# The inverse of the chunk matrices as pairs of 64x64 tiles: one step of a hybrid diffusion backbone

## The reference, cut to what matters

```
low = jnp.where(strict, jnp.einsum('bhncd,bhnsd->bhncs', kb, k) * decay, 0.0)
tmat = lax.linalg.triangular_solve(eye + low, jnp.broadcast_to(eye, low.shape), left_side=True, lower=True)
u = tmat @ vb
w = tmat @ (kb * jnp.exp(g)[..., None])
def step(s, inp):                      # over the chunks
    v_new = u_i - w_i @ s
    o_i = q_i @ s + qk_i @ v_new
    s = s * gl_i[..., None, None] + jnp.einsum('bhcd,bhce->bhde', k_i, v_new)
```

## Time and profile before

| | us |
|---|---|
| median of 3 runs | 8628.4 |
| lowest, highest | 8619.2, 8630.4 |
| span of the profiled execution | 8614.4 |
| PE busy with matmuls | 6895.8 (80%) |
| PE busy with weight loads | 5819.8 (68%) |
| DVE busy | 4241.4 (49%) |
| ACT busy | 1628.0 (19%) |
| POOL busy | 290.5 (3%) |

### The profile page before, as it was taken

The page is one execution under the profiler, slowest core; times in us unless marked ns, Lnnn a source line. Parts: engine busy times, 40 slices in busy tenths (PEclk is TensorE's granted clock), DMA queues, the critical chain, the costliest instruction groups (busy, mean ns, idle before and its releaser), DMA issues. The chain is left out here.

```text
span 8614.4 us, 112116 instructions
## 1 busy us (share of the span) xinstructions
PE 6895.8 (80%) x44860; PEld 5819.8 (68%) x44860; DVE 4241.4 (49%) x7492; ACT 1628.0 (19%) x2928; POOL 290.5 (3%) x260
## 2 busy tenths in 40 slices
PE   7788888888798677798945676699678887888698
PEld 1666666666698555697944565599566666666698
DVE  0446666666434422434156666433546666666433
ACT  0211111111222122323221111222211111111322
POOL 0000000000000000000000000000000000000000
PEclk9899999999899777899977787799888888888899
DMA  6221111110221200221311000121110000000121
GB/s 244 78 76 38 38 38 39 38 38 32 73 73 47 77 16 16 74 78 49 113 51 37 25 19 20 64 70 60 65 50 9 9 9 9 9 9 3 68 78 56
DMA packets 96935, 429.11 MB, mean 50 GB/s; under 512 B 16041, under 2 KB 26537, under 8 KB 64873
## 3 DMA queue, kind: packets, MB, share of 16 engines
q1 hardware_dynamic: 83248, 392.92, 12.9%
q10 hardware_dynamic: 13248, 30.15, 0.9%
HBM read 374.03 MB, written 49.26 MB: 49 GB/s over the span
## 5 line engine op out<-in xcount | busy, mean ns | idle before, releaser
L343 PE MATMUL bank<-src_hi,ring_hi 128*128 128x320 f32 x4032 | 936.6, 314 | 358.9 <-DVE ring_lo L335 354.9
L343 PE MATMUL bank<-src_lo,ring_hi 128*128 128x320 f32 x4032 | 933.3, 313 | 7.4 <-issue 7.4
L343 PEld LDWEIGHTS bank<-src_hi,ring_hi 128*128 128x128 f32 x4032 | 688.4, 192 | 362.8 <-issue 358.2
L343 PE MATMUL bank<-src_hi,ring_lo 128*128 128x320 f32 x4032 | 932.5, 313 | 0.0
L343 PEld LDWEIGHTS bank<-src_lo,ring_hi 128*128 128x128 f32 x4032 | 688.6, 192 | 7.8 <-issue 7.8
L343 PEld LDWEIGHTS bank<-src_hi,ring_lo 128*128 128x128 f32 x4032 | 687.6, 191 | 0.0
L335 DVE TENSOR_TENSOR ring_lo<-ring,ring_hi 128x2048 fp32r<-128x2048 f32 x190 | 434.9, 2289 | 508.6 <-ACT ring_hi L331 507.7
L735 PE MATMUL bank<-xx,y 128*128 128x128 f32 x3200 | 522.6, 286 | 75.5 <-DVE y L768 56.3
L779 DVE TENSOR_TENSOR xx<-bank,xx 128x512 f32<-128x512 f32 x600 | 414.7, 691 | 289.0 <-PE bank L739 289.0
L768 DVE TENSOR_TENSOR y<-bank,const 128x256 f32<-128x256 f32 x1000 | 416.1, 421 | 283.3 <-PE bank L727 277.4
L727 PE MATMUL bank<-xx,lt 128*128 128x128 f32 x3200 | 501.5, 288 | 26.1 <-DVE xx L779 26.1
(11 more groups left out here) (354 smaller groups left out, 11469.4 us busy)
## 6 DMA issues: line engine op xcount, KB each, us to landing
ring<-w_mlp SPq DMA_DIRECT2D x128, 1024.0 KB, 4.8
mod_ring<-w_mod SPq DMA_DIRECT2D x24, 2048.0 KB, 7.7
mod_slab<-w_mod SPq DMA_DIRECT2D x24, 2048.0 KB, 7.6
ring<-rw_wrkv SPq DMA_DIRECT2D x24, 1024.0 KB, 4.7
ring<-dn_win SPq DMA_DIRECT2D x16, 1024.0 KB, 5.2
rkv<-stage ACTq DMA_DIRECT2D x48, 320.0 KB, 2.2
rkv<-rkv SPq DMA_DIRECT2D x48, 320.0 KB
rows<-dn_rows SPq DMA_DIRECT2D x8, 1920.0 KB, 6.8
```

Of the source, the lines that this page charges most:

```text
L343: last = self.nc.tensor.matmul(acc[h][:, 0:HALF], wt[:, n % 2, k, m * P:(m + 1) * P], x[:, k, h * HALF:(h + 1) * HALF], start=first and q ...
```

## The change

The zeros beside the diagonal blocks are no longer kept. `lt`, `xx`, `y`, `x0` and `tt` have 128 rows of 64 columns: rows 0 to 63 are the block of one direction, rows 64 to 127 that of the other. Each product of two 128x128 matrices becomes two products of 64x64 (SIDES), one on rows 0 to 63 into partitions 0 to 63, one on rows 64 to 127 into partitions 64 to 127 of the same PSUM bank. The DVE instructions of the inverse have half as many columns; their masks are tables of 64 columns. The start's transposes are products with the identity, thus two records each. The product from which `lt` comes is formed in 64 columns too: in time mixing by 64x64 tiles on the rows of one head, in the delta heads by 128x64 tiles over all rows, and its mask there runs by sides (64 partitions of 256 columns) where it ran by heads (128 partitions of 256 columns). The product with `tt` in the chains runs as pairs of tiles of 64x64 with all its 128 columns moving. All waits of PE ahead of such tiles become `wait_alone`.

```diff
-    t[:, K_L0:K_L0 + P] = (row // 2 == col // 2) & (col > row)
+    row, col = r[:, None] % C, r[None, :C]
+    t[:, K_SPC:K_SPC + C] = col > row
+    t[:, K_L0:K_L0 + C] = (row // 2 == col // 2) & (col > row)
+    t[:, K_IDC:K_IDC + C] = row == col
...
+SIDES = (slice(0, C), slice(C, P))
...
 def invert_first_pe(pe, nc, g, s, w, i, j, h):
-    pe.wait_ge(s["first_t"], group_at(i, j, "first_t", h + 1))
+    wait_alone(pe, s["first_t"], group_at(i, j, "first_t", h + 1), s["passed"])
     for n in range(2):
-        last = nc.tensor.transpose(w.y_bank[h][:, (2 + n) * P:(3 + n) * P], w.x0[h][:, 1, n, :], g.ident)
+        for er in SIDES:
+            last = nc.tensor.matmul(w.y_bank[h][er, (2 + n) * C:(3 + n) * C], w.x0[h][er, 1, n, :], g.ident[er, er],
+                                    start=True, stop=True)
...
-            pe.wait_ge(s["xx_ready"], group_at(i, j, "xx_ready", 2 * lv + h + 1))
+            wait_alone(pe, s["xx_ready"], group_at(i, j, "xx_ready", 2 * lv + h + 1), s["passed"])
...
             for n in range(2):
-                last = nc.tensor.matmul(w.y_bank[h][:, n * P:(n + 1) * P], w.lt[:, j % 2, 2 * h + n, :], xx[h][:, 0, n, :],
-                                        start=True, stop=True)
+                for er in SIDES:
+                    last = nc.tensor.matmul(w.y_bank[h][er, n * C:(n + 1) * C], w.lt[er, j % 2, 2 * h + n, :],
+                                            xx[h][er, 0, n, :], start=True, stop=True)
...
-            pe.wait_ge(s["ly_ready"], group_at(i, j, "ly_ready", 2 * lv + h + 1))
             if lv == 0 and j:
-                pe.wait_ge(s["inv_ready"], group_at(i, j - 1, "inv_ready", h + 1))
+                wait_alone(pe, s["inv_ready"], group_at(i, j - 1, "inv_ready", h + 1), s["passed"])
+            wait_alone(pe, s["ly_ready"], group_at(i, j, "ly_ready", 2 * lv + h + 1), s["passed"])
             for n in range(2):
-                last = nc.tensor.matmul(w.x_bank[h][:, (2 + n) * P:(3 + n) * P], w.y[:, h, n, :], xx[h][:, 1, n, :],
-                                        start=True, stop=True)
+                for er in SIDES:
+                    last = nc.tensor.matmul(w.x_bank[h][er, (2 + n) * C:(3 + n) * C], w.y[er, h, n, :], xx[h][er, 1, n, :],
+                                            start=True, stop=True)
...
-                nc.vector.tensor_tensor(both, w.x_bank[h][:, :], before, ALU.add).then_inc(s["xx_ready"], 1)
+                nc.vector.tensor_tensor(both, w.x_bank[h][:, 0:4 * C], before, ALU.add).then_inc(s["xx_ready"], 1)
...
-        w.lt, w.xx, w.y = sb("lt", 2, GROUP, P), sb("xx", 2, 2, 2, P), sb("y", 2, 2, P)
+        w.lt, w.xx, w.y = sb("lt", 2, GROUP, C), sb("xx", 2, 2, 2, C), sb("y", 2, 2, C)
...
                         hr = slice(C * hh, C * (hh + 1))
-                        for q, (left, right) in enumerate(((bt, at_), (kt, at_), (kt, rt), (bt, rt))):
+                        for n in range(2):
+                            u = 2 * jg + n
+                            for e, er in enumerate(SIDES):
+                                nc.tensor.matmul(bank[4 + 2 * hh][er, n * C:(n + 1) * C], bt[hr, u, e, :], at_[hr, u, e, :],
+                                                 start=True, stop=True)
+                        for q, (left, right) in enumerate(((kt, at_), (kt, rt), (bt, rt)), 1):
...
-                        pe.wait_ge(s["x_out"], at(i, 2 * STEPS, 2 * n + 2))
+                        wait_alone(pe, s["x_out"], at(i, 2 * STEPS, 2 * n + 2), s["passed"])
                         for hh, uk in enumerate(uks):
-                            last = nc.tensor.matmul(bank[1][:, hh * P:(hh + 1) * P], w.tt[:, uk, :],
-                                                    xs[:, hh, :].unsqueeze(1).to_broadcast([P, 2, C]), start=True, stop=True)
+                            for er in SIDES:
+                                last = nc.tensor.matmul(bank[1][er, hh * P:(hh + 1) * P], w.tt[er, uk, :],
+                                                        xs[er, hh, :].unsqueeze(1).to_broadcast([C, 2, C]),
+                                                        start=True, stop=True)
...
+                            if b == 0:
+                                for er in SIDES:
+                                    last = nc.tensor.matmul(bank[0][er, n * C:(n + 1) * C], k2[:, hh, u, er], k2[:, hh, u, er],
+                                                            start=True, stop=True)
...
-                        pe.wait_ge(s["tmp_out"], at(i, STEPS, n + 1))
+                        wait_alone(pe, s["tmp_out"], at(i, STEPS, n + 1), s["passed"])
```

84 lines of the change are left out of this document (49 added, 35 removed).

## The result

The changed kernel takes 8176.4 us (median of 3 runs, 8171.3 to 8185.3) against 8628.4: ratio 0.948, 95% interval 0.9464 to 0.9498. The forecast was 8050: of 582 us less, span to span, 445 came. The result lies in the stated range (7940 to 8450), but 16 us above the range that the forecast's own bounds gave (7940 to 8160). The page of the changed kernel first: span, busy time, the queue that fetches instructions, and the two lines of y and x products.

A forecast was written before the change was run, and what follows sets the result against it. It took TensorE's instruction stream to bound the inverse's levels. The inverses save 601 us and the chains add 19, so the span falls from 8614.4 to 8032; with 14 around it 8046, stated as 8050. Range 7940 to 8450.

The forecast's parts named there:

- Price of a pair, 0.12: In the inverse, a pair of 64x64 products takes 0.12 us where one 128x128 product took 0.22; bounds 0.11 and 0.22.
- Rival (b): The two tiles of a pair don't overlap: 8560 us, or 8700 with dearer waits and pairs; chance 0.12.
- DVE, 415 and 283 ns: In the inverse, VectorE's sum falls from 691 to 415 ns and the mask from 421 to about 283.
- the ring: Half 0's loop in a quiet level: x products, sum, wait, y products, mask, wait; 2.20 us against 3.28 before.
- The wait, 0.135: In the inverse, PE's separate wait makes loads start 0.135 us behind DVE's end; bounds 0.05 and 0.22.
- The levels, 3.73, 3.74, 2.20, 4.34, 1.64: Time-mixing heads, us for each level of a group after the change; before, modelled 5.15, 5.07, 3.15, 6.35, 2.33.
- the walk: Following all 25 levels of a block by dependence: 105.5 us before, 74.6 after; delta heads 94.2 and 67.5.
- rival (c): Instruction supply to TensorE doesn't hold 46 per us in the inverse; at 30 the kernel takes 8730 us; chance 0.05.
- rival (a): TensorE's clock in the inverse is no longer granted in full; near 8400 us; chance 0.12.
- A: Theory from the experiments, not the prediction: the clock falls because the narrow tiles leave PE too thinly used.
- The chain, +19: The tt product's change of form and wait add 16 us (0 to 32) in 160 chain steps, 3 in 40 delta steps.
- Around the span, 14 us: Before the change, the runs' median 8628.4 us stood 14 above the profiled span; added to 8032 to give 8046.

The follow-up runs named there:

- e4: Changed kernel with each of the 800 VectorE sums writing its 256 columns twice, so 512 as before; 8279 us, ratio 0.9607 to the kernel before.
- e3: Kernel before with only the waits of the inverse changed, each made an instruction of its own; 8653 us, ratio 1.0036 to the kernel before.
- e8: Changed kernel with 8 more TensorE instructions per level that only count up a semaphore; 8176 us, ratio 0.9480 to the kernel before.
- e9: Changed kernel with 64 semaphore-counting TensorE instructions ahead of the loop of each time-mixing phase, shifting the code; 8121 us, ratio 0.9416 to the kernel before.
- e1: Changed kernel with unread 128x128 products over 96 columns put into TensorE's idle spots of the inverse; 8346 us, ratio 0.9686 to the kernel before.
- e6: Changed kernel with unread pairs of 64x64 bf16 tiles of 256 columns as fills in TensorE's idle spots of the inverse; 8156 us, ratio 0.9462.
- e2: Changed kernel with lt, xx, y and x0 of the inverse in bf16, one TensorE record per tile in place of two; 8017 us, ratio 0.9301.
- e7: Changed kernel with the inverse in bf16 and one unread pair of 64x64 bf16 tiles as fill in each idle spot; 8033 us, ratio 0.9312.
- e11: Changed kernel with the inverse in bf16 and two unread pairs of tiles as fill in each of 900 places; 7981 us, ratio 0.9259.
- e10: Changed kernel with unread pairs of 64x64 tiles as fills and 2 + 2 semaphore counts per level; 8111 us, ratio 0.9415 to the kernel before.

## Why the prediction came out as it did

- **Price of a pair, 0.12**: 0.115. The tiles of a pair start 0.035 us apart and overlap though both write one PSUM bank. Rival (b) is out. The Trainium skill (TensorEngine Tiling (Array Packing), Gotcha 1) says that different row tiles can't use one bank at a time; 0.115 us a pair, where one behind the other would take 0.22, doesn't bear that out for two tiles that write different partitions of the bank.
- **DVE, 415 and 283 ns**: 425 and 290. That the sum is on the ring is shown by e4, at some 75 us.
- **The wait, 0.135**: 0.11 to 0.12 behind DVE's end. e3 prices a wait that lies on the path at 0.075 us, about what 0.135 less 0.055 makes.
- **The levels, 3.73, 3.74, 2.20, 4.34, 1.64**: 3.76, 3.78, 2.19, 4.30, and 1.70 to 1.90. A block without pause and low clock takes, by estimate from the quietest blocks, 76.7 us (forecast 74.6) and 70.9 in the delta heads (67.5). In the time-mixing heads the walk was short by as much for before (105.5 against 108.5), so the difference held; in the delta heads it was short by 3.4 after and 0.3 before. Undisturbed, the inverses would have fallen by 2132 - 16 x 76.7 - 4 x 70.9 = 621 us; the term was 601. Most of the difference is that layer 3's blocks took 110.8 before and not the 108.5 that the walk was held against.
- **What failed: rival (c) was sized as all or nothing.** I asked whether the supply holds 46 instructions per us and gave it 0.05, at a price of 8730. It does not hold everywhere: 60 us of pauses at a few fixed places. No level became slower throughout. e8 and e9 show that the rate per level was the wrong measure: more instructions gave fewer pauses, and a shift of 64 halved them. What empties the supply at such a place stays open: e9 shows that place matters, not how. A wait attached to the loads of a pair, which would save those instructions, wasn't tried.
- **What failed: rival (a), the clock, was counted as a rival of the whole and not as a term.** Low clock in the inverses 216 us against 43, worth about 70 us (what is left of 1641 - 60 of pauses - 1511 undisturbed). Half of the falls come behind pauses; when only the idle time is filled they stay in e1 (19) and go to 10 in e6. The other half goes with filling. e2, e3, e7 and e11 show falls with no pause of supply near. e8 is not explained by A: PE is used no more there, and the falls without a pause still went from 17 to 5. So what makes the clock fall is shown in part only. I took the 88% busy share as safe; a share of busy time that counts the tails of matmuls says little for the clock (0.61 at 91% in e11). The Trainium skill has a second passage on this (TensorE: Matmul & The Clock Gate, "A second HAM failure mode"), on short idle spells between groups of matmuls, with which the clock swings between its two levels; the changed kernel's trace agrees in that its clock falls 35 times in the inverses and comes back each time, behind spells of at most 2.4 us.
- **The chain, +19**: +77, of which 66 in the time-mixing heads. Its steps were right: 4.76 where 4.77 was forecast in layer 0, 3.88 where 3.79 stood before in layer 3, 6.93 where 6.83 stood in the delta heads. Where the chain starts at full clock (e10) the time-mixing chains take 18 us more than before, against 16 forecast. The other 48 us go with low clock that the inverse hands over: 118 us of it in the changed kernel, 7 in e10. So rival (a) is missing from the sum a second time.
- **The rest, 0**: -32, of which 21 are the accident of the profile before. That part is luck. The other 11 lie in the work between the blocks and were not looked into.
- **Around the span, 14 us**: there is no such term. The profiled execution of the changed kernel took 8171.3 us against a span of 8169.5, 1.8 apart; the 14 was the spread of the runs of before.

Sum: 621 - 60 - 70 - 77 + 32 = 446, where 445 came. The mechanism (the ring with the shorter sum, mask and pairs) was right; the two terms left out are worth some 180 us, and some of that was made good by 20 us of underrated gain and the 32.

Of the prediction's signs, the pair, the DVE times, the wait, the quiet level and the chain step came as written. The clock did not stay at 1.00, part of PE's idle time is put down to issue, and 4 of the 20 blocks stay above 85 us (88.1 to 90.3) where their mean is 82.

## What to carry to other kernels

When a change takes work from an engine by giving it more and shorter instructions, put two terms into the sum and not into the rivals: pauses in which the instructions don't come, and a lower clock, also in the work that follows. Where TensorE waits in short spells, products whose result nobody reads can help to hold the clock. Here they were free in the form of tile that stands around them (e6) and cost more than they gave in another (e1). After such a change shift the code by some instructions and time it again before you judge a difference under 1%.

## What I had not expected of the hardware

- 64 idle instructions ahead of two loops: 8176 to 8121 us.
- Three fills in another tile form cost a level three times 0.27 us; three in the form around them nothing that the level shows (2.20 us).
- An instruction that only counts up a semaphore takes 0.15 us in PE's sequencer, and eight more of them a level took most pauses away (52 to 6).
- The clock fell to half for 17 us behind a pause of 1.5 us, with PE busy for 94% of those 17.
- An inverse at half clock throughout in bf16 (75 us) is faster than in f32 at full clock (79 us): there TensorE is hardly the bound any more.
- The half clock that the inverse leaves behind doubles the first chain step, 4.67 to 8.4 us, in a stretch that has other instructions.
